# A steady product behind the sums of every attention step, and a buffer of their own for the meta tokens' queries

## What is computed

```python
def stick_breaking(q, k, v, q_pos, k_pos, bias):
    z = einsum('bqhd,bkhd->bhqk', q, k) * DH_A ** -0.5 + bias
    mask = k_pos[None, :] < q_pos[:, None]
    log_keep = where(mask, log_sigmoid(-z), 0.0)
    later = cumsum(log_keep, axis=3, reverse=True) - log_keep
    att = where(mask, exp(log_sigmoid(z) + later), 0.0)
    return einsum('bhqk,bkhd->bqhd', att, v)
# RWKV-7, token by token: state = state*w - (state.kk)(kk*a) + v k ;  y = state.r
```

## Time and profile before

| | |
|---|---|
| median of 3 runs | 3437.68 us (3432.95 to 3444.43) |
| the profiled execution | 3451.49 us, of it 3449.8 us span |
| mixers stage, attention and recurrence | about 495 to 1157 us of the span |
| TensorE busy, whole kernel | 3274.4 us (95%) |
| granted TensorE clock, mean over the kernel | 0.958 |
| DVE, ACT, POOL busy | 58%, 39%, 19% |

### The profile page before, as it was taken

One profiled execution on the slowest core, in us unless ns is written; L12 is line 12 of the kernel. 1 busy time (PEld: TensorE's weight loads), 2 busy tenths in 40 slices (PEclk: granted clock), 3 DMA queues, 4 the chain that ended last, 5 costly groups with the idle time before them and its releaser, 6 DMA issues. The chain is left out here.

```text
span 3449.8 us, 56008 instructions
## 1 busy us (share of the span) xinstructions
PE 3274.4 (95%) x20556; PEld 2956.9 (86%) x20556; DVE 2007.6 (58%) x3776; ACT 1342.5 (39%) x2645; POOL 664.3 (19%) x1026
## 2 busy tenths in 40 slices
PE   8999988989899999999999999999889999999998
PEld 7999756656566799999999989998579999999997
DVE  6444436566657686555555566533668655555555
ACT  5444334555555663222322244213456322232223
POOL 0000122333333051111111021001215111111102
PEclk9999986889889999999999999999989999999999
DMA  5333472323222351111111312233434211111131
GB/s 151 129 128 128 149 240 84 100 55 103 53 58 50 98 173 62 53 45 43 44 53 43 125 27 70 84 123 120 168 102 144 72 49 43 48 43 54 43 124 52
DMA packets 371571, 304.76 MB, mean 88 GB/s; under 512 B 74413, under 2 KB 333873, under 8 KB 371396
## 3 DMA queue, kind: packets, MB, share of 16 engines
q1 hardware_dynamic: 356168, 249.95, 24.1%
q0 software_dynamic: 14080, 50.45, 4.1%
q10 hardware_dynamic: 1152, 2.11, 0.2%
HBM read 223.09 MB, written 79.37 MB: 88 GB/s over the span
## 5 line engine op out<-in xcount | busy, mean ns | idle before, releaser
L1515 PE MATMUL ffn_ps<-parts_hi,ffn_w_lo 128*128 128x368 f32 (+2 forms) x1152 | 379.2, 329 | 0.0
L1513 PE MATMUL ffn_ps<-parts_hi,ffn_w_hi 128*128 128x368 f32 (+2 forms) x1152 | 378.9, 329 | 0.0
L481 PE MATMUL ffn_ps<-ffn_h_hi,ffn_w_hi 128*128 128x368 f32 (+2 forms) x1008 | 336.1, 333 | 9.0 <-DVE ffn_h_lo L1150 5.4
L483 PE MATMUL ffn_ps<-ffn_h_hi,ffn_w_lo 128*128 128x368 f32 (+2 forms) x1008 | 332.9, 330 | 0.0
L482 PE MATMUL ffn_ps<-ffn_h_lo,ffn_w_hi 128*128 128x368 f32 (+2 forms) x1008 | 332.2, 330 | 0.0
L1514 PE MATMUL ffn_ps<-parts_lo,ffn_w_hi 128*128 128x368 f32 (+2 forms) x1008 | 331.1, 328 | 0.0
L1268 DVE TENSOR_TENSOR mix<-ffn_ps,mix 128x368 f32<-128x368 f32 (+2 forms) x432 | 229.7, 538 | 148.0 <-PE ffn_ps L483 148.0
L872 ACT ACTIVATE ffn_w_hi<-ffn_sums 128x512 fp32r<-128x512 f32 x144 | 84.7, 624 | 472.4 <-PE ffn_ps L483 359.7
L481 PE MATMUL ffn_ps<-parts_hi,ffn_w_hi 128*128 128x368 f32 (+2 forms) x768 | 257.9, 336 | 2.9 <-DVE ffn_w_lo L1078 2.9
L482 PE MATMUL ffn_ps<-parts_lo,ffn_w_hi 128*128 128x368 f32 (+2 forms) x768 | 253.7, 330 | 0.0
L483 PE MATMUL ffn_ps<-parts_hi,ffn_w_lo 128*128 128x368 f32 (+2 forms) x768 | 252.8, 329 | 0.0
(11 more groups left out here) (592 smaller groups left out, 8128.3 us busy)
## 6 DMA issues: line engine op xcount, KB each, us to landing
out_w_first<-in_w_ffn_gate_dram SPq DMA_DIRECT2D x44, 512.0 KB, 3.8
ffn_w_raw<-in_w_ffn_up_dram SPq DMA_DIRECT2D x44, 512.0 KB, 3.9
first_w_raw<-in_w_in_ab_dram SPq DMA_DIRECT2D x27, 512.0 KB, 4.0
out_w_first<-in_w_ffn_down_dram SPq DMA_DIRECT2D x22, 512.0 KB, 3.5
ffn_w_raw<-in_w_ffn_down_dram SPq DMA_DIRECT2D x22, 512.0 KB, 3.4
rwkv_prep<-xT POOLq DMA_DIRECT2D x4, 2208.0 KB, 7.5
qkv_proj<-head_out_sb POOLq DMA_DIRECT2D x16, 552.0 KB, 3.6
atts_v_page<-in_cache_v_dram POOLq DMA_DIRECT2D x32, 256.0 KB, 6.1
```

The lines of the kernel that those rows point to most:

```text
L481: pe.matmul(out, w_hi, x_hi, start=first, stop=False)
L483: return pe.matmul(out, w_lo, x_hi, start=False, stop=last)
L1513: pe.matmul(out, w[0], x_hi, start=first and k == 0, stop=False, skip_group_check=True)
L1515: mm = pe.matmul(out, w[1], x_hi, start=False, stop=k == HALF - 1, skip_group_check=True)
```

## The change

`scores(n)` now notes in a list that it was issued. `steady(n)` waits until ACT has emptied the bank Z of the last scores issued (none before the first) and puts n products of `idle_products` into that bank. It is called with 4 behind `strict 1`, 4 ahead of and 6 behind `tokens 0`, 2 at each of the seven items `first`, and 1 behind `sums` of every attention step. The meta tokens' queries get a buffer and a semaphore of their own; the two halves of `q_in` alternate between long blocks alone. The next long block is asked for at the first step of the present long one, and a pair's meta queries right behind that at the pair's second long block.

```diff
+    LONG = len(q_blocks)
+    long_starts = [n for n in block_starts if steps[n][2] == G]
+    long_at = [sum(n <= t for n in long_starts) - 1 for t in range(NS)]
...
+        q_meta = s.sb("q_meta", [P, 2, 2, N_META], F32R)
+        meta_loaded = s.sem("meta_loaded")
...
             def load_q(b):
-                i, q0, width = steps[block_starts[b]][0:3]
+                i, q0, width = steps[long_starts[b]][0:3]
...
+            def load_meta(i):
+                for x in range(2):
+                    for half in range(2):
+                        sp.dma_start(q_meta[pair(half), x, :, :].bitcast(F32), query(i, x, 0, N_META)
+                                     ).then_inc(meta_loaded, 16)
...
-                    if part == 0 and 0 < t < NS and first[t] and block_at[t] + 1 < len(block_starts):
+                    if part == 0 and 0 < t < NS and t in long_starts:
                         sp.wait_ge(z_mm, t)
                         part_waits(sp, parted)
-                        load_q(block_at[t] + 1)
+                        if long_at[t] + 1 < len(long_starts):
+                            load_q(long_at[t] + 1)
+                        if long_at[t] % LONG == 1:
+                            load_meta(i)
...
+            scored = []
+            def steady(n):
+                if scored:
+                    pe.wait_ge(z_scaled, 2 * len(scored))
+                    part_waits(pe, parted)
+                idle_products(pe, c, att[:, Z, :, :].rearrange("p x n -> p (x n)"), n)
...
                     if kind == "strict":
                         strict(item[1])
+                        if item[1] == 1:
+                            steady(4)
+                    elif kind == "first":
+                        steady(2)
...
                     elif kind == "tokens":
                         g = item[1]
+                        if g == 0:
+                            steady(4)
                         post_bank(last_use)
                         tokens(g)
+                        if g == 0:
+                            steady(6)
...
-                b = block_at[n]
+                b = long_at[n]
+                of_block = q_in[:, b % 2, :, :, :] if width == G else q_meta[:, :, :, :]
                 if first[n]:
-                    pe.wait_ge(q_loaded[b % 2], (b // 2 + 1) * 64)
+                    if width == G:
+                        pe.wait_ge(q_loaded[b % 2], (b // 2 + 1) * 64)
+                    else:
+                        pe.wait_ge(meta_loaded, 64 * (i + 1))
...
                         sums(t - 2)
+                        steady(1)
```

More of the change, by code:

```diff
@@ L2942, in load_v_low, with query @@
                              ).then_inc(v_loaded[1], 16)
+            def query(i, x, q0, width):
+                at = ((2 + x) * NPAIR + i) * P
+                return qk_parts[at:at + P, q0:q0 + width].rearrange("(h d) t -> d h t", d=DH)
             def load_q(b):
-                i, q0, width = steps[block_starts[b]][0:3]
+                i, q0, width = steps[long_starts[b]][0:3]
                 for x in range(2):
-                    at = ((2 + x) * NPAIR + i) * P
-                    of = qk_parts[at:at + P, q0:q0 + width].rearrange("(h d) t -> d h t", d=DH)
                     for half in range(2):
-                        sp.dma_start(q_in[pair(half), b % 2, x, :, 0:width].bitcast(F32), of).then_inc(q_loaded[b % 2], 16)
+                        sp.dma_start(q_in[pair(half), b % 2, x, :, :].bitcast(F32), query(i, x, q0, width)
+                                     ).then_inc(q_loaded[b % 2], 16)
+            def load_meta(i):
[3 more added lines that the diff above has]
+                                     ).then_inc(meta_loaded, 16)
             def load_gate(i):
@@ L3405, in scores @@
                         mm = pe.matmul(att[0:keys, Z, hh, lo:width], k_in[:, hh, k0:k0 + keys],
-                                       q_in[:, b % 2, x, hh, lo:width], start=x == 0, stop=x == 1 and not diag,
+                                       of_block[:, x, hh, lo:width], start=x == 0, stop=x == 1 and not diag,
                                        skip_group_check=True)
@@ L3411, in scores @@
                 mm.then_inc(z_mm, 1)
+                scored.append(n)
             def sums(n):
```

## The result

| | before | after |
|---|---|---|
| median | 3435.31 us (3428.98 to 3444.43, 4 runs) | 3488.00 us (3478.99 to 3493.07, 4 runs) |
| ratio, 95% interval | | 1.0148 (1.0114 to 1.0183) |
| profiled execution, span | 3449.8 us | 3490.5 us |
| granted clock, whole kernel | 0.958 | 0.973 |

The changed kernel is slower by 1.5%, 51 us. The forecast was slower, 22 us; the time lies in its range, but the loss is more than twice the forecast.

A forecast was written before the change was run, and what follows sets the result against it. The prediction took TensorE, with a clock often low in the mixers stage, as the bound. Its terms, +54 + 10 - 40 - 2 = +22 us on the median of 3437.7, gave 3460 us, range 3415 to 3500.

The forecast's parts named there:

- The bound: Mixers stage: TensorE sets the pace, busy 585 of 662 us, with a clock often at its lower level.
- A: Products behind `sums`: 100 at 0.86 us make 86 us, 32 hidden in waits, so +54 us.
- B: Stage's start, 28 products: second `gather` 13 us later, less 3 for the raised clock, so +10 us.
- C: Low clock outside the start: 0.65 of 168 us goes, 109 us at 0.37 each, so -40 us.
- D: Third pair's queries, asked for three steps earlier: the 1.97 us wait of `scores` goes, so -2 us.
- It balances: Rival, whole change: 50 us hidden, 0.65 of low time gone, start +10; +4 us, 3442 us; chance 0.21.
- The clock is not bought: Rival, steps: a quarter of low time goes, 20 us of waits filled; +63 us, 3501 us; chance 0.18.
- The clock pays: Rival, behind the start: 50 us of waits filled, 0.95 of 168 us gone; -19 us, 3419 us; chance 0.24.

The follow-up runs named there:

- e3: Against the kernel before: the queries' part and the 100 products behind `sums`, none at the start; 3477.58 us, 1.0104.
- e1: Against the kernel before: only the queries' buffer and moved loads, no steady product and no added wait; 3439.91 us, 1.0001.
- e4: Against the kernel before: the queries' part and the added wait for the emptied scores' bank behind `sums`, no product issued; 3444.19 us, 1.0006.
- e2: Against the kernel before: the queries' part and the 28 products of the start, none behind `sums`; 3456.58 us, 1.0041.
- e7: Against the kernel before: the queries' part and 29 products (14.6 us) inside round trips, none elsewhere; 3432.95 us, 0.9980.
- e11: Against the kernel before: the queries' part and only 20 half-width products between each `gather` and its `tokens`; 3432.50 us, 0.9976.
- e12: Against the kernel before: the same kernel as e7, run once more; 3435.52 us, 0.9991.

## Why the prediction fell short, point by point

- **The bound.** Right. TensorE sets the pace: where the clock is full, a step grew by 0.85 us for a product of 0.86 (5.6 us for a step were forecast, 5.76 found).
- **A, the 100 products: +54 forecast, +60 found** (e3 against e1, at equal clock: 57.5 + 2.7). 32 us were to be hidden, 26 were. Most of the waits named in the prediction did shrink. The wait of `tokens` did not shrink at all; the prediction had left 7 us of it out as a round trip, rightly, but counted 3.4 us as fillable. The added wait was put at nothing: e4 has it at 1 us behind `sums`, and in the start the products waited 2.9 us.
- **B, the start: +10 forecast, +16 found** (e2 against e1, in time). Of the positions only the last was near. The first scores were put near 514 and came at 509.39: the first products were to run at the low clock, which no row showed, and they ran at full clock from 496.11. The inverse was to start 5 us late and started 1 us late, but lost 7 us more on the way, by caps that wait for scores. So +9.7 for the second `gather`, where +13 less 3 was forecast, is in part luck. The balance was then drawn at 529 us, as if nothing were lost behind it. The runs have 6 us more at the end; 10 us of low time that come back would be some 3.5 us of it (an estimate), and the rest is open. The 5.71 us wait that was to take some of the products took little: 4 of 24 us were hidden.
- **C, the clock: -40 forecast, about -25 found for the steps.** The price of a low microsecond was right, 0.37 forecast and 0.35 found. Its amount was not: 109 us of low time were to go with the products behind `sums`, 68 to 72 went. This is the largest error, 15 of the 28 us that are missing; A and B have 6 each, the queries the last one. Some of it is the stock. The profile that gave the 168 us has 290 us of low time in the whole kernel, 24 more than the mean of 266. With 144 us the share of 0.65 would have given 94 us and -35 (an estimate); the measured 72 of 144 are a half. The rest of the error is that share. The reason given for it, that a product fills most of a 1 us wait, holds only for waits that can be filled, and the wait of `tokens`, 11.1 us in e3, can't be filled from behind `sums`. That falls of the clock hang on such waits fits e7, e11 and e12, where low time falls by 25 to 29 us with products inside them and by 13 with the same amount elsewhere; single falls were not traced to single waits.
- **D, the queries: -2 forecast, -1.3 found,** not to be told from nothing.
- **The rivals.** "It balances" took the forecast's C with 50 us hidden, and neither came. "The clock is not bought" named the right weakness (the clock is missing where TensorE waits for others), and with 50 us the result lies between it and the forecast, nearer to the rival. "The clock pays" asked for 108 us of low time with 50 us hidden; it got 82 to 93 with 26 to 30.
- **The rule of the Trainium skill** ("TensorE: Matmul & The Clock Gate", HAM oscillation), half of every throttled microsecond, would make of the 93 us a gain of 46 us, where the 0.35 us of 103 executions makes 33. The measurement decides here. The likely reason, that TensorE's waits for other engines don't shorten with its clock, was not tested by itself.

## What to carry to other kernels

A filler matmul that is to hold the clock has a price in full where TensorE sets the pace, here 0.85 us for 0.86, and the clock's return must be read from how much low time it can reach, not from how much there is. Put it inside a round trip, right ahead of the instruction that waits for the other engine's answer and no longer than that wait, and see that it has nothing to wait for itself: 20 half products there gave 0.9976 (0.9960 to 0.9992), 100 whole ones behind every step 1.0104. The gain is small, a fifth of a percent here. Filler at a start must be judged by the time of the whole kernel and not by the clock of the start: 27 us of low time went there, 14 to 18 in all. And a stock of low time belongs to one execution; take it from several.

## What was not expected of the hardware

Most of the scatter of this one-core kernel, 3423 to 3452 us, goes with how long TensorE's clock was at the lower level, from 226 to 297 us, with the same program and the same data. A single profile can therefore mislead by as much as a small change is worth: the profiled execution of before was 14 us above its median, and against it the profiled changed kernel was 41 us slower, not 51.
